# Turns in two sequence mixers: transposes in place of products with the identity

## The chip, the cores and the metric

The kernel runs on one core of one Trainium2 chip. The metric is the device time of one execution in microseconds. The kernel before took 2492.74 us (median of 3 runs, 2491.64 to 2497.43).

## What is computed

Two transformer blocks, one behind the other, on 256 tokens of width 2048, all in float32. The first block's middle part is a pair of recurrent mixers; the second block's is an attention with a forget gate. Only the first block's mixers matter here:

```python
def first_block(x, ...):
    h = rms_norm(x, attn_norm_w[l])
    proj = h @ w_cat                                   # 2048 -> 6448
    y_a, v_first = rwkv7_mixer(p_rwkv, ...)            # 16 heads of 64
    y_b = gdn_mixer(p_gdn, ...)                        # 8 value heads of 128, 4 key heads
    y = jnp.concatenate([y_a, y_b], axis=-1)
    x = x + y @ w_out[l]
    h = rms_norm(x, ffn_norm_w[l])
    x = x + (silu(h @ ffn_w_gate[l]) * (h @ ffn_w_up[l])) @ ffn_w_down[l]
```

The first mixer keeps for each head a 64 x 64 state that every token updates:

```python
def step(S, inp):                                      # rwkv7_recurrence
    Sa = einsum('bhvk,bhk->bhv', S, a_t)
    S = S * w_t + Sa[..., None] * b_t + v_t[..., None] * k_t
    return S, einsum('bhvk,bhk->bhv', S, r_t)
```

The second is the gated delta rule in chunks of 64 tokens: `v_new = u - w @ S`, `o = q_g @ S + A_qk @ v_new`, `S = S * exp(g_last) + k_g.T @ v_new`, where `u` and `w` solve a unit lower triangular system `L + I` of 64 x 64. The kernel computes both mixers in chunks of 64 tokens, with products and an inverse of such a triangular matrix in place of the token by token scan.

## The kernel before

Activations lie channel by channel on the 128 partitions, with the 256 tokens along the free axis. The large products (`unit`, L1921; its three products are L1952 to L1954) stream all weights once from memory through a ring of 4 slots; each weight is split by ScalarE (L606) and VectorE (L1076) in a high and a low part, and three products make one. Their phases are: input projection (to about 305 us), mixers (305 to 545 us), output projection, FFN, then the second block. Each engine runs its own program in written order; semaphores join them.

Inside the mixers the weight slots are used as work space and TensorE runs many small products. Two heads of 64 channels share a tile of 128 partitions: `halves_of` (L2092) holds the slices 0 to 63 and 64 to 127, and most small products are issued as a pair, one for each half. `C` is 64, `P` 128, `T` 256, `PAIRS` 8 (pairs of heads of the first mixer), `NCH` 4 (chunks), `G_QK` 4 (key heads of the second).

The chunk algorithm needs many 64-token blocks turned (channels to tokens or back). A turn is a product with the identity matrix `ident`: the block is the stationary operand, `ident` the moving one, and the result lands in PSUM. The turns, in the order in which TensorE comes to them:

- the fills: `chunk_tokens` (L2094, product at L2097) turns values, b and k of a chunk, 12 calls of 8 pairs; `chunk_turn` (L2109, product at L2113) turns the start of the inverse, 4 calls of 8 pairs. The list `FILLS` mixes these calls with `chunk_scores` (L2106, a real product) over the 8 PSUM banks, each fill waiting for the bank's eviction eight fills earlier;
- five levels of the first inverse (L2144, L2152, L2156), no turns;
- the first mixer's scan over 4 chunks (L2194 to L2243), into which `value_tokens` (L2172) is woven in chunks 1 and 2: 4 pairs a call, each pair reading all 128 partitions and writing one half;
- the turn of `GT` at L2249 (16 pairs), then five levels of the second inverse (L2259, L2275, L2279), with `key_tokens` (L2165) in four of them and `value_tokens` in two, 4 pairs a call;
- `turned_heads` (L2289), the first mixer's output back to channels, 4 calls of 8 pairs: two ahead of the second mixer's scan, two in its first step;
- `turned_values` (L2312), the second mixer's output back, 4 calls of 4 full 128 x 128 blocks, in steps 2 and 3 of that scan and behind it.

ACT evicts most turns (L820, L824, L841, L864, L888); each call signals once, on its last instruction. Elsewhere in the kernel (x at the start L2012, small vectors L2007 and L2026, the attention L2414 and L2422, the end L2459) blocks are turned by `nc.tensor.transpose`, which takes the same operands.

Of the kernel before, what the change touches and what calls it, by code (L numbers as in the profile page):

```python
# [24 lines left out]
P = 128  # L25
T = 256
# [3 lines left out]
C = 64  # L30
# [13 lines left out]
INV_BANKS, SIDE_BANKS = (7, 1, 5, 0), (2, 6, 4, 3)  # L44
STATE_BANKS, O_BANKS, TURN_BANKS, Y_BANKS = (1, 5), (7, 4), (6, 3), (2, 6, 3, 2)
# [40 lines left out]
def build(nc, io, out):  # L86
    with ExitStack() as ctx:
# [39 lines left out]
        ident = at("ident", [P, P], o); o += 512  # L127
# [52 lines left out]
        YT = at("YT", [P, NCH, PAIRS, C], a3 + 16384)  # L180
# [14 lines left out]
        TT = at("TT", [P, SLOTS, C], w0)  # L195
# [20 lines left out]
        QC, KC, VC = QKVC[:, 0:4, :], QKVC[:, 4:8, :], QKVC[:, 8:16, :]  # L216
# [11 lines left out]
        GT = at("GT", [P, NCH, 2, G_QK, C], w0)  # L228
# [10 lines left out]
        OT = at("OT", [P, NCH, G_QK, P], a3 + 8192)  # L239
# [37 lines left out]
        ps = [ctx.enter_context(nc.psum_tensor(f"ps{i}", [P, 512], F32)) for i in range(8)]  # L277
# [1637 lines left out]
        def _(pe):  # L1915
            mm = nc.tensor.matmul
# [86 lines left out]
            for n in range(NT):  # L2003
# [5 lines left out]
                for q in range(4):  # L2009
                    for i in range(4):  # L2010
                        f = 4 * q + i
                        ins = nc.tensor.transpose(ps[4 * n + q][:, i * P:(i + 1) * P], XIN[:, n, f * P:(f + 1) * P],  # L2012
                                                  ident[:])
                    ins.then_inc(S("x_turned"), 1)

            for j in range(4):
                if j == 3:
                    pe.wait_ge(S("vecs_landed"), counts["vecs_landed"])
                    for i, pack in list(enumerate(PACKS))[1:]:
                        r = sum(n for _, n in pack)  # L2020
                        b = 3 + (i - 1) % 5
# [15 lines left out]
            for name, r, b0 in (("w_lora", slice(0, 64), 0), ("a_lora", slice(64, 128), 4)):  # L2037
                for t in range(PAIRS):
                    pe.wait_ge(bank_freed, N_OUT - 8 + b0 + t // 2 + 1 + FREE_BANKS)
                    ins = mm(ps[b0 + t // 2][:, (t % 2) * T:(t % 2 + 1) * T], WA_UP[r, t * P:(t + 1) * P],  # L2040
                             PR[r, T_WA, PAD:TP], start=True, stop=True)
# [27 lines left out]
            for t in range(PAIRS):  # L2069
                o_ = ps[4 + t // 2][:, (t % 2) * T:(t % 2 + 1) * T]  # L2070
                mm(o_, G_UP[:, 0, t * P:(t + 1) * P], PR[:, T_G0, PAD:TP], start=True, stop=False)
                ins = mm(o_, G_UP[:, 1, t * P:(t + 1) * P], PR[:, T_G1, PAD:TP], start=False, stop=True)
# [5 lines left out]
            for c in range(NCH):  # L2078
                for e, rr in enumerate((slice(0, C), slice(C, P))):
                    ins = mm(ps[0][rr, 16 * c:16 * c + 16], ROWS[:, c * C:(c + 1) * C], picks[:, e, :, 0, :],  # L2080
                             start=True, stop=True)
# [9 lines left out]

            halves_of = (slice(0, C), slice(C, P))  # L2092

            def chunk_tokens(dst, src, c):  # L2094
                for t in range(PAIRS):
                    for rr in halves_of:
                        ins = mm(dst[rr, t * C:(t + 1) * C], src[rr, t, c * C:(c + 1) * C], ident[rr, rr],  # L2097
                                 start=True, stop=True)
                ins.then_inc(S("tok_turned"), 1)

            def chunk_scores(dst, src, q):
# [7 lines left out]
            def chunk_turn(dst, c):  # L2109
                got("tt_started")  # L2110
                for t in range(PAIRS):
                    for rr in halves_of:
                        ins = mm(dst[rr, t * C:(t + 1) * C], TT[rr, 8 * c + t, :], ident[rr, rr], start=True, stop=True)  # L2113
                ins.then_inc(S("tm_turned"), 1)

            k_hat, v_in = (PR[:, t:t + PAIRS, PAD:TP] for t in (T_K, T_V))
# [2 lines left out]
            for fill, kind in enumerate(FILLS):  # L2119
# [4 lines left out]
                dst, i = ps[fill % 8], place[kind]  # L2124
# [12 lines left out]
            for lev in range(1, 6):  # L2137
                for b in range(NCH):
# [3 lines left out]
                    for t in range(PAIRS):  # L2142
                        for rr in halves_of:
                            ins = mm(ps[2 * b][rr, t * C:(t + 1) * C], LO[rr, 8 * b + t, :], TM[rr, 8 * b + t, :],  # L2144
                                     start=True, stop=True)
                    ins.then_inc(S("inv_p"), 1)
                for b in range(NCH):
                    got("inv_pm")
                    if lev < 5:
                        for t in range(PAIRS):  # L2150
                            for rr in halves_of:
                                mm(ps[2 * b][rr, t * C:(t + 1) * C], TT[rr, 8 * b + t, :], PM[rr, 8 * b + t, :],  # L2152
                                   start=True, stop=True)
                    for t in range(PAIRS):
                        for rr in halves_of:
                            ins = mm(ps[2 * b + 1][rr, t * C:(t + 1) * C], PM[rr, 8 * b + t, :], TT[rr, 8 * b + t, :],  # L2156
                                     start=True, stop=True)
# [4 lines left out]
            def key_tokens(c, b):  # L2162
                for a in range(G_QK):
                    for rr in halves_of:
                        ins = mm(ps[b][rr, a * P:(a + 1) * P], KC[:, a, c * C:(c + 1) * C], ident[:],  # L2165
                                 start=True, stop=True)
                ins.then_inc(S("tok_turned"), 1)

            def value_tokens(c, b):
                for a in range(G_QK):  # L2170
                    for e, rr in enumerate(halves_of):
                        ins = mm(ps[b][rr, a * P:(a + 1) * P], VC[:, 2 * a + e, c * C:(c + 1) * C], ident[:],  # L2172
                                 start=True, stop=True)
                ins.then_inc(S("tok_turned"), 1)

            def gram(c):
# [6 lines left out]
            for c in range(NCH):  # L2183
                cc = slice(c * C, c * C + C)
                s0 = ST[:, c % 2]
                for hb in range(2):
                    if c:
                        got("s_out")
                    for i in range(4):
                        t = 4 * hb + i  # L2190
# [4 lines left out]
                        for rr in halves_of:  # L2195
                            ins = mm(o_[rr], LKR[rr, 8 * c + t, 0, :], VTOK[rr, 8 * c + t, :], start=c == 0, stop=True)
# [11 lines left out]
                for hb in range(2):  # L2208
# [3 lines left out]
                    for i in range(4):  # L2212
                        t = 4 * hb + i
                        for rr in halves_of:
                            ins = mm(ps[2 + 4 * hb][rr, i * C:(i + 1) * C], TT[rr, 8 * c + t, :], R1[rr, t, :],
                                     start=True, stop=True)
                    ins.then_inc(S("u_summed"), 1)
                for hb in range(2):
# [3 lines left out]
                    for i in range(4):  # L2222
                        t = 4 * hb + i
# [3 lines left out]
                        for rr in halves_of:  # L2227
                            ins = mm(o_[rr], BTOK[rr, 8 * c + t, :], UU[rr, t, :], start=False, stop=True)
# [6 lines left out]
                for t in range(PAIRS):  # L2235
# [6 lines left out]
                    for rr in halves_of:  # L2242
                        ins = mm(o_[rr], LBR[rr, 8 * c + t, 1, :], UU[rr, t, :], start=False, stop=True)  # L2243
                ins.then_inc(S("y_summed"), 1)
            for c in range(NCH):
                got("gtt_start")
                for a in range(G_QK):
                    for rr in halves_of:
                        ins = mm(ps[INV_BANKS[c]][rr, a * C:(a + 1) * C], GT[rr, c, 1, a, :], ident[rr, rr],  # L2249
                                 start=True, stop=True)  # L2250
                ins.then_inc(S("tm_turned"), 1)

            for lev in range(1, 6):
                for c in range(NCH):
                    got("inv_off")
                    got("inv_added" if lev > 1 else "tm_made")
                    for a in range(G_QK):
                        for rr in halves_of:
                            ins = mm(ps[INV_BANKS[c]][rr, a * C:(a + 1) * C], gLO[rr, c, a, :], GT[rr, c, 0, a, :],  # L2259
                                     start=True, stop=True)  # L2260
# [8 lines left out]
                for c in range(NCH):  # L2269
                    got("inv_pm")  # L2270
                    b = INV_BANKS[c]
                    if lev < 5:
                        for a in range(G_QK):
                            for rr in halves_of:
                                mm(ps[b][rr, a * C:(a + 1) * C], GT[rr, c, 1, a, :], gPM[rr, c, a, :],  # L2275
                                   start=True, stop=True)
                    for a in range(G_QK):
                        for rr in halves_of:
                            ins = mm(ps[b][rr, T + a * C:T + (a + 1) * C], gPM[rr, c, a, :], GT[rr, c, 1, a, :],  # L2279
                                     start=True, stop=True)  # L2280
# [4 lines left out]
            def turned_heads(e):  # L2285
                for t in (2 * e, 2 * e + 1):
                    for k in range(NCH):
                        for rr in halves_of:
                            ins = mm(ps[Y_BANKS[e]][rr, (t % 2) * T + k * C:(t % 2) * T + (k + 1) * C],  # L2289
                                     YT[rr, k, t, :], ident[rr, rr], start=True, stop=True)  # L2290
                ins.then_inc(S("y_turned"), 1)
            for c in range(NCH):
                got("inv_added")
                for a in range(G_QK):
                    for rr in halves_of:
                        ins = mm(ps[INV_BANKS[c]][rr, a * P:(a + 1) * P], GT[rr, c, 1, a, :], VB[rr, c, a, :],
                                 start=True, stop=True)
# [11 lines left out]
            def turned_values(c):  # L2309
                got("o_out")  # L2310
                for a in range(G_QK):
                    ins = mm(ps[TURN_BANKS[c % 2]][:, a * P:(a + 1) * P], OT[:, c, a, :], ident[:], start=True, stop=True)  # L2312
                ins.then_inc(S("o_turned"), 1)

            def state_sums(c, vn):
# [29 lines left out]
            for c in range(1, NCH):  # L2345
                vn = VN[:, c % 2, :, :]
                got("gs_out", 2)
                for a in range(G_QK):
                    for e, rr in enumerate(halves_of):
                        ins = mm(ps[0][rr, a * P:(a + 1) * P], WT[:, c, e, a, :], gS[c % 2][:, 4 * e + a, :],  # L2350
                                 start=True, stop=True)
# [126 lines left out]
```

## Time and profile before

| | |
|---|---|
| median of 3 runs | 2492.74 us (2491.64 to 2497.43) |
| the profiled execution | 2492.21 us, of which the span of the profile 2490.4 us |
| TensorE busy (MATMUL) | 2436.8 us, 98% of the span, 24650 records |
| VectorE, ScalarE, GpSimd busy | 59%, 45%, 5% |
| mean granted TensorE clock | 0.995 of full |
| memory traffic | 431.72 MB, 173 GB/s |

Times are those of one profiled execution, in us unless marked ns. PE is TensorE's MATMUL, PEld its weight load, DVE VectorE, ACT ScalarE, POOL GpSimd. A FP32 product shows as two MATMUL records, each with a load of its own. "64*128 64x64" is the form of a record: 64 rows and 128 columns of the array hold the stationary operand, and a moving operand of 64 partitions x 64 elements goes through. Ends of MATMULs are modelled and overlap the next one's start, so rates are read from starts: in a row of the timeline, "start us, us" is the first start and the time to the last end. PEclk 1.00 is 2.4 GHz.

### The profile page before, as it was taken

Reading aid. Unit: us, or ns where it says so; the run is one execution under the profiler, and the core shown is the slowest. Engines: PE = TensorE matmul, PEld = TensorE weight load, DVE = VectorE, ACT = ScalarE, POOL = GpSimd, SP = SyncE. Lnnn points to the kernel's source line nnn. Section 1 sums busy time; section 2 is a strip of 40 time slices with the busy share of each in tenths; the row PEclk is TensorE's granted clock in tenths of the full one; section 3 lists DMA queues with packets and bytes.
Section 4 is the critical chain, followed back from the end, with each engine's and each line's share of the span. In section 5 each row is a group of like instructions: output and inputs, shape, how many; then the busy total and the mean of one; then the engine's idle time right before and its main releaser. Section 6 shows DMA issues by size and latency. Waiting matters only on the chain.

```text
span 2490.4 us, 57362 instructions
## 1 busy us (share of the span) xinstructions
PE 2436.8 (98%) x24650; PEld 2409.6 (97%) x24650; DVE 1477.9 (59%) x1683; ACT 1122.8 (45%) x1061; POOL 114.4 (5%) x93
## 2 busy tenths in 40 slices
PE   8999979989999999999999999999999999999999
PEld 8999968989999999999999999989999999999998
DVE  5557598664654545554445567675576666765444
ACT  4333524444544444443344544363555555544332
POOL 3000050000200000000020100000200000000000
PEclk9999989999999999999999999999999999999999
DMA  7555300126555655556665565626565565656664
GB/s 233 186 188 199 119 2 4 37 86 186 194 195 188 198 186 194 193 189 196 189 197 192 186 237 202 218 78 197 187 196 192 189 198 186 196 191 190 198 188 150
DMA packets 171387, 431.72 MB, mean 173 GB/s; under 512 B 17614, under 2 KB 23387, under 8 KB 170107
## 3 DMA queue, kind: packets, MB, share of 16 engines
q1 hardware_dynamic: 170027, 422.30, 52.3%
q10 hardware_dynamic: 1232, 7.52, 0.8%
q8 instruction: 104, 1.70, 0.3%
q14 instruction: 24, 0.20, 0.0%
HBM read 427.59 MB, written 2.17 MB: 173 GB/s over the span
## 4 chain that ended last, share of the span: by engine, by line
PE 92%; DVE 6%; ACT 1%; POOL 1%; issue 0%; DMA 0%; DVEq 0%; SPq 0%; ACTq 0%; POOLq 0%
PE ps L1952 29%; PE ps L1953 29%; PE ps L1954 29%; PE ps L2106 1%; POOL SQ L528 1%; DVE TM L1351 0%; DVE LO L1355 0%; DVE TT L1352 0%; DVE CV L1385 0%; ACT HIW L606 0%; DVE LOW L1076 0%; DVE GT L1367 0%; PE ps L2144 0%; DVE TMP L1298 0%; PE ps L2050 0%
## 5 line engine op out<-in xcount | busy, mean ns | idle before, releaser
L1076 DVE TENSOR_TENSOR LOW<-RAW,HIW 128x2048 fp32r<-128x2048 f32 (+1 forms) x397 | 912.8, 2299 | 916.4 <-ACT HIW L606 916.3
L1952 PE MATMUL ps<-H_ROWS,HIW 128*128 128x256 f32 x4928 | 1369.1, 278 | 6.3 <-DVE LOW L1076 3.6
L1953 PE MATMUL ps<-H_ROWS,HIW 128*128 128x256 f32 x4928 | 1368.0, 278 | 0.0
L1954 PE MATMUL ps<-H_ROWS,LOW 128*128 128x256 f32 x4928 | 1367.1, 277 | 0.0
L606 ACT ACTIVATE HIW<-RAW 128x2048 fp32r<-128x2048 f32 (+1 forms) x397 | 760.9, 1917 | 1182.7 <-PE ps L1954 1178.2
L1952 PEld LDWEIGHTS ps<-H_ROWS,HIW 128*128 128x128 f32 x4928 | 927.9, 188 | 7.6 <-DVE LOW L1076 4.0
L1954 PEld LDWEIGHTS ps<-H_ROWS,LOW 128*128 128x128 f32 x4928 | 929.2, 189 | 0.0
L1953 PEld LDWEIGHTS ps<-H_ROWS,HIW 128*128 128x128 f32 x4928 | 927.5, 188 | 0.1
L1952 PE MATMUL ps<-HID,HIW 128*128 (+1 forms) x1408 | 389.3, 276 | 0.0
L1953 PE MATMUL ps<-HID,HIW 128*128 (+1 forms) x1408 | 389.2, 276 | 0.0
L1954 PE MATMUL ps<-HID,LOW 128*128 (+1 forms) x1408 | 389.1, 276 | 0.0
L1952 PEld LDWEIGHTS ps<-HID,HIW 128*128 128x128 f32 x1408 | 264.4, 188 | 0.2 <-issue 0.2
L1954 PEld LDWEIGHTS ps<-HID,LOW 128*128 128x128 f32 x1408 | 264.4, 188 | 0.0
L1953 PEld LDWEIGHTS ps<-HID,HIW 128*128 128x128 f32 x1408 | 264.4, 188 | 0.0
L528 POOL TENSOR_TENSOR NSQ<-NSQ 128x1024 f32<-128x1024 f32 (+2 forms) x12 | 26.2, 2187 | 502.9 <-ACT NSQ L634 502.3
L1896 DVE SCALAR_TENSOR_TENSOR YV<-UC,vec,YV 128x256 f32<-128x256 f32 x88 | 42.5, 483 | 0.0
L1896 DVE SCALAR_TENSOR_TENSOR YG<-UC,vec,YG 128x256 f32<-128x256 f32 x88 | 42.5, 483 | 0.0
L528 POOL TENSOR_TENSOR SQA<-SQA 128x1024 f32<-128x1024 f32 (+1 forms) x4 | 9.8, 2460 | 603.7 <-ACT SQA L640 603.6
L1120 DVE TENSOR_TENSOR UC<-ps,rstd 128x256 f32<-128x256 f32 x88 | 30.1, 418 | 0.0
L648 ACT ACTIVATE H_ROWS<-X,vec 128x256 fp32r<-128x256 f32 x64 | 27.0, 494 | 0.0
L1115 DVE SCALAR_TENSOR_TENSOR H_ROWS<-X,vec,H_ROWS 128x256 fp32r<-128x256 f32 x64 | 26.8, 479 | 0.0
L1045 ACT ACTIVATE YV<-UC,vec 128x256 f32<-128x256 f32 x44 | 25.9, 588 | 0.0
(365 smaller groups left out, 1507.0 us busy)
## 6 DMA issues: line engine op xcount, KB each, us to landing
RAW<-in_ffn_w_up SPq DMA_DIRECT2D x264, 512.0 KB, 4.5
RAW<-in_ffn_w_down SPq DMA_DIRECT2D x176, 512.0 KB, 4.8
RAW<-in_fox_w_in SPq DMA_DIRECT2D x98, 512.0 KB, 4.6
RAW<-in_w_in SPq DMA_DIRECT2D x96, 512.0 KB, 4.2
RAW<-in_ffn_w_gate SPq DMA_DIRECT2D x88, 512.0 KB, 3.8
RAW<-in_w_out SPq DMA_DIRECT2D x32, 512.0 KB, 5.0
RAW<-in_fox_w_out SPq DMA_DIRECT2D x32, 512.0 KB, 4.7
INV<-rows_out ACTq DMA_DIRECT2D x4, 1024.0 KB, 7.2
```

The costliest lines, as they stand in the source:

```text
L528: tick(nc.gpsimd.tensor_tensor(sq[:, 0:n, :], sq[:, 0:n, :], sq[:, n:2 * n, :], ALU.add), "pool_step")
L606: A(HIW[:, u_const % 2, 0:n], RAW[:, u_const % 4, 0:n], ACT.Copy).then_inc(hi_made, 1)
L648: A(H(0, f, f + 1)[:, 0, :], X[:, f, :], ACT.Copy, scale=vec[:, c + f:c + f + 1]).then_inc(S("h_hi"), 1)
L1045: ins = A(conv_out(i), UC[:, i, 0:T], ACT.Identity, scale=conv_tap(g, 0, i), bias=vec[:, bass.ds(g * 4 + (cb + (i % 2) * FT + i // 2), 1)])
L1076: V.tensor_tensor(LOW[:, u_const % 4, 0:n], RAW[:, u_const % 4, 0:n], HIW[:, u_const % 2, 0:n].bitcast(F32), ALU.subtract).then_inc(lo_mad ...
L1115: V.scalar_tensor_tensor(H(1, f, f + 1)[:, 0, :], X[:, f, :], vec[:, c + f:c + f + 1], H(0, f, f + 1)[:, 0, :].bitcast(F32), ALU.mult, ALU ...
L1120: return V.tensor_tensor(dst, ps[f][:, 0:T], rstd[:], ALU.mult)
L1896: ins = V.scalar_tensor_tensor(conv_out(i), UC[:, i, j - 1:j - 1 + T], conv_tap(g, j - 1, i), conv_out(i), ALU.mult, ALU.add)
L1952: mm(o_, hi_w, h_hi, start=start, stop=False)
L1953: mm(o_, hi_w, h_lo, start=False, stop=False)
L1954: i = mm(o_, lo_w, h_hi, start=False, stop=stop)
L2106: ins = mm(dst[rr, i * P:(i + 1) * P], src[rr, t, cc], AR[rr, t, :, cc], start=True, stop=True)
```

## The change

Every turn of the mixers' main part whose result starts at partition 0 becomes `nc.tensor.transpose`; its partner, which lands on partitions 64 to 127, stays a product. The second mixer's turned values, which are full blocks, all become transposes. Nothing else is moved; the operands, the order, the waits and the signals stay. (`picks`, `spread_inverse` and the real products are untouched.)

```diff
+            def turned(dst, src, rr, unit_matrix):
+
+                if rr.start == 0:
+                    return nc.tensor.transpose(dst[rr], src, unit_matrix)
+                return mm(dst[rr], src, unit_matrix, start=True, stop=True)
+
             def chunk_tokens(dst, src, c):
                 for t in range(PAIRS):
                     for rr in halves_of:
-                        ins = mm(dst[rr, t * C:(t + 1) * C], src[rr, t, c * C:(c + 1) * C], ident[rr, rr],
-                                 start=True, stop=True)
+                        ins = turned(dst[:, t * C:(t + 1) * C], src[rr, t, c * C:(c + 1) * C], rr, ident[rr, rr])
                 ins.then_inc(S("tok_turned"), 1)
...
-                        ins = mm(dst[rr, t * C:(t + 1) * C], TT[rr, 8 * c + t, :], ident[rr, rr], start=True, stop=True)
+                        ins = turned(dst[:, t * C:(t + 1) * C], TT[rr, 8 * c + t, :], rr, ident[rr, rr])
...
-                        ins = mm(ps[b][rr, a * P:(a + 1) * P], KC[:, a, c * C:(c + 1) * C], ident[:],
-                                 start=True, stop=True)
+                        ins = turned(ps[b][:, a * P:(a + 1) * P], KC[:, a, c * C:(c + 1) * C], rr, ident[:])
...
-                        ins = mm(ps[b][rr, a * P:(a + 1) * P], VC[:, 2 * a + e, c * C:(c + 1) * C], ident[:],
-                                 start=True, stop=True)
+                        ins = turned(ps[b][:, a * P:(a + 1) * P], VC[:, 2 * a + e, c * C:(c + 1) * C], rr, ident[:])
...
-                        ins = mm(ps[INV_BANKS[c]][rr, a * C:(a + 1) * C], GT[rr, c, 1, a, :], ident[rr, rr],
-                                 start=True, stop=True)
+                        ins = turned(ps[INV_BANKS[c]][:, a * C:(a + 1) * C], GT[rr, c, 1, a, :], rr, ident[rr, rr])
...
-                            ins = mm(ps[Y_BANKS[e]][rr, (t % 2) * T + k * C:(t % 2) * T + (k + 1) * C],
-                                     YT[rr, k, t, :], ident[rr, rr], start=True, stop=True)
+                            ins = turned(ps[Y_BANKS[e]][:, (t % 2) * T + k * C:(t % 2) * T + (k + 1) * C],
+                                         YT[rr, k, t, :], rr, ident[rr, rr])
...
             def turned_values(c):
                 got("o_out")
                 for a in range(G_QK):
-                    ins = mm(ps[TURN_BANKS[c % 2]][:, a * P:(a + 1) * P], OT[:, c, a, :], ident[:], start=True, stop=True)
+                    ins = nc.tensor.transpose(ps[TURN_BANKS[c % 2]][:, a * P:(a + 1) * P], OT[:, c, a, :], ident[:])
                 ins.then_inc(S("o_turned"), 1)
```

## Rows read from the trace of the kernel before

**Rows 1.** The page, part 1: busy time and share of the span.

```profile
PE 2436.8 (98%) x24650; PEld 2409.6 (97%) x24650; DVE 1477.9 (59%) x1683; ACT 1122.8 (45%) x1061; POOL 114.4 (5%) x93
```

**Rows 2.** The page, part 4: the chain that ended last, by engine.

```profile
PE 92%; DVE 6%; ACT 1%; POOL 1%; issue 0%; DMA 0%; DVEq 0%; SPq 0%; ACTq 0%; POOLq 0%
```

**Rows 3.** That chain in order of time, 335 to 565 us: start us, us, what.

```profile
360.13 1.15 PE ps L2097 x32
...
367.58 3.75 PE ps L2113 x128
...
443.43 1.02 PE ps L2172 x16
...
472.43 1.87 PE ps L2249 x64
...
476.17 1.02 PE ps L2165 x16
...
484.49 0.87 PE ps L2172 x16
...
518.19 2.01 PE ps L2289 x64
...
521.22 2.01 PE ps L2289 x64
```

**Rows 4.** TensorE's waits, 339 to 372 us: total us, times, longest.

```profile
PE ps L2097 <- DVE LKR L1441: 0.6, 1, 0.6
```

**Rows 5.** Single lines of TensorE: min/median/max ns, first and last start, forms.

```profile
L2097 PE MATMUL ps<-ident,PR x256: 215/218/268, 348.4 to 366.5; 64*64 64x64 f32 x128
...
L2289 PE MATMUL ps<-ident,YT x128: 217/219/268, 518.1 to 523.0; 64*64 64x64 f32 x128
...
L2165 PE MATMUL ps<-ident,PR x64: 272/273/323, 476.1 to 500.4; 128*64 128x128 f32 x64
```

**Rows 6.** The same for the full-width turn L2312 and for two transposes.

```profile
L2312 PE MATMUL ps<-ident,OT x32: 274/275/377, 527.6 to 544.1; 128*128 128x128 f32 x32
...
L2422 PE MATMUL ps<-ident,SC x48: 272/273/329, 1640.1 to 1669.5; 128*128 128x128 f32 x48
...
L2026 PE MATMUL ps<-ident,VPACK x7: 223/272/297, 29.2 to 30.4; 88*128 88x88 f32 x4, 67*128 67x67 f32 x1, 83*128 83x83 f32 x1, 64*128 64x64 f32 x1
```

**Rows 7.** Timeline of TensorE: start us, us to the last end, instructions.

```profile
483.40 1.09 PE L2165 MATMUL ps<-ident,PR 128*64 128x128 f32 x16
484.32 1.04 PE L2172 MATMUL ps<-ident,PR 128*64 128x128 f32 x16
485.30 0.68 PE L2275 MATMUL ps<-gPM,GT 64*64 64x64 f32 x16
...
515.16 1.09 PE L2331 MATMUL ps<-U,AL 64*64 64x128 f32 x16
516.18 2.00 PE L2304 MATMUL ps<-GT,KBE 64*128 64x64 f32 x32
518.12 2.08 PE L2289 MATMUL ps<-ident,YT 64*64 64x64 f32 x64
```

**Rows 8.** The same timeline at the end of the mixers; in brackets the idle time before.

```profile
539.19 1.16 PE L2312 MATMUL ps<-ident,OT 128*128 128x128 f32 x8 [0.33 <-ACT OT L888]
543.23 1.16 PE L2312 MATMUL ps<-ident,OT 128*128 128x128 f32 x8 [2.88 <-ACT OT L888]
```

**Rows 9.** Three stretches: length, busy by engine, PEclk, DMA share, GB/s.

```profile
348.30:372.00 23.70, 22.41 (x646) 22.13 (x642) 21.25 (x36) 10.28 (x17) 12.07 (x9) 1.00 0.02 4
541.50:544.90 3.40, 1.16 (x8) 0.97 (x8) 1.95 (x6) 3.07 (x10) 0.00 (x0) 1.00 0.00 0
544.90:551.70 6.80, 6.02 (x28) 6.03 (x29) 3.97 (x6) 1.90 (x3) 0.00 (x0) 0.50 0.00 0
```

**Rows 10.** Timeline of TensorE at the start: 16 transposes twice.

```profile
6.26 3.27 PE L2012 MATMUL ps<-ident,XIN 128*128 128x128 f32 x16 [6.26 <-DMA XIN<-in_x]
...
9.62 1.97 PE L2012 MATMUL ps<-ident,XIN 128*128 128x128 f32 x16
```

## The prediction

> **What bounds the kernel now.** I read the page's busy shares first, then the chain of work that ended last, then that chain in order of time through the two mixers of the first block (335 to 545 us), and only then single lines. TensorE is busy for 98% of the span [rows 1] and carries 92% of the chain [rows 2]; nearly all of that is the large products, which the change does not touch. What it touches lies in the mixers. There the reader should see in the chain that the turns are on it almost everywhere: the fills (L2097, L2113), the value and key turns (L2172, L2165), the turn of GT (L2249) and both pairs of head turns (L2289) [rows 3]. In the fills, 339 to 372 us, TensorE stood idle only once behind its first start, 0.6 us on a DVE mask product [rows 4]. So a nanosecond more or less on a turn is a nanosecond of the kernel, and the price of one turn decides.
>
> **How a pair of turns runs today.** A turn comes as a pair: the half on partitions 0 to 63 and the half on 64 to 127. Each product is two MATMUL records (16 products of a call give 32 records), and its form is 64*64: 64 rows, 64 columns of the array [rows 5]. One 128-wide record of L2312 follows the next after (1.16 - 0.28 - 0.10) / 7 = 0.11 us (1.16 us for 8 records, less the tail of the last, 0.275, and what the first is longer than the median, 0.377 - 0.275 [rows 6, 8]), so a 64-wide one should take 0.055. But L2113 runs 128 records in 3.75 us, 0.029 each [rows 3]: the two halves, in opposite corners of the array, run at the same time. A narrow pair costs 4 x 0.029 = 0.117 us, set equally by either half. A wide pair (L2165, L2172: form 128*64, 128 moving columns) costs 0.217: 0.87 us for the four of a call [rows 3].
>
> **What the change does to a pair.** The lower half becomes one transpose, the upper stays a product. Counts: 8 pairs in each of 12 token fills and 4 TT turns (128 pairs), 16 in GT, 32 in the heads: 176 narrow. The wide ones are 4 pairs in 8 calls: 32. Each loses one MATMUL and one weight load of four.
>
> First, the length of a transpose. Sixteen transposes at the start take 1.97 us [rows 10]: less the last one's tail (0.273) and the first one's extra (0.055) that is 0.11 us each, against 0.22 for a product of that size in two records. It saves half. (The Trainium skill, "TensorE: Matmul & The Clock Gate", section Terms, calls transpose mode four times faster for FP32; the rows disagree, showing a factor of two. By the page a narrow transpose would take 0.027 instead of 0.055, and the sum below would be 6.5 us less.)
>
> But halving one half alone wins nothing even in the best case: the upper half still needs its two records of 0.055, and they set the pace of a pair that runs side by side. The lower bound of a pair is thus about 0.11, as now.
>
> Second, and this decides: can it still run side by side? No row shows a transpose that uses fewer than 128 columns of the array. The forms are 128*128, 88*128, 83*128, 67*128, and even the one with 64 rows and a 64x64 moving matrix is 64*128 [rows 6]; all of them had 128 stationary columns, so this is a hint and no proof. The helper's own condition is the second hint: it transposes only where the output starts at partition 0. An operation that could live in a 64*64 corner could live in either; one that takes the full width can only start at the left edge. I take the new instruction as 64*128 (128*128 in the wide turns), so it alternates with products of form 64*64 (128*64). (The Trainium skill, "TensorEngine Tiling (Array Packing)", Restrictions, says the same: column tiling disables transpose mode for FP32 input. No row here can confirm it.)
>
> Third, what alternating between forms costs. The timeline of TensorE has such changes, now only between calls. L2172 starts at 484.32 and L2275, another form, at 485.30: 0.98 us for four pairs that cost 0.87, where nothing is waited for, so about 0.10 for leaving the form. L2165 before it, which changes the form on entry and not at its end, takes 0.92: 0.05 for the first load that nothing hides [rows 7]. The medians agree: the first record after a change is 0.05 longer (268 against 218, 323 against 272 [rows 5]). The pair of forms that matters here is there too: L2331 (64*64) gives way to L2304 (64*128) after 1.02 us for four pairs of 0.217, again 0.15 over [rows 7]. So a change costs 0.15 in all: 0.10 to empty the array and 0.05 for the load. (The same page of the Trainium skill, Key Properties, says that changing the tiling mode drains TensorE; the trace agrees, and has the price that the page lacks.) Before a transpose the bare load is cheaper: 128 columns are 0.055 longer (329 against 273) where a product's are 0.10 (377 against 275) [rows 6]; for 64 columns I take 0.027.
>
> A narrow pair afterwards, start to start: transpose 0.027 load + 0.055 + 0.10 to empty = 0.182; first product record 0.05 + 0.055 = 0.105; second 0.055 + 0.10 = 0.155. Sum 0.44 against 0.117: **+0.325 us**. A wide pair, with 0.11 in place of 0.055: 0.237 + 0.16 + 0.21 = 0.607; a call of four 2.43 against 1.02 [rows 3], **+1.40 us**.
>
> **The sum.**
> - Fills (L2097, L2113): 128 x 0.325 = 41.6, less the 0.6 us of idle time that swallows the start of it [rows 4]: +41.0. The ACT and DVE evictions behind each fill keep their length and have more time.
> - Turn of GT: 16 x 0.325 = +5.2. On the chain as a whole [rows 3].
> - Key and value turns: 8 x 1.40 = +11.2. L2172 at 443 and 452 us lies in a stretch where TensorE has no gap; in the levels of the inverse TensorE goes from these calls straight on to L2275 without waiting, so it was the later one and the delay passes on.
> - Head turns: 32 x 0.325 = 10.4, less the 0.15 by which each of the two stretches' entries is a change of form already: +10.1.
> - Second mixer's turned values: 16 products of 0.22 become transposes of 0.11, -0.44 us of TensorE in each of four calls, -1.8 in all. These are full width, with no alternation. But L2312 is nowhere on the chain; before two of the calls TensorE has stood idle for ACT, 2.88 us before the last [rows 8]. I price it at 0. If all were exposed it would be 1.8.
>
> No wait is added, the signal of each call stays on its last instruction, and no DMA or queue moves. Sum: 41.0 + 5.2 + 11.2 + 10.1 = **+67.5 us**. On the profiled execution (2492.2 us, of which 2490.4 span) that is 2559.7; the median of the runs is 0.5 above it, so **2560 us**.
>
> Bounds of the pair, the one unknown price: from below 0.055 x 3 = 0.165 (in turn, but without emptying the array): 176 x 0.048 + 32 x 0.11 = +12 us in all; if a transpose loads as slowly as a full product (0.10) the pair is 0.51 and the sum 13 us more. Nearest are the L2331 to L2304 rows, which have the very two forms.
>
> **Rivals.**
> 1. *The clock falls in the turns.* The granted clock was 1.00 from 348 to 372 us with TensorE nearly gapless; it was 0.50, the 1.2 GHz level, in 544.9 to 551.7, right behind a stretch with 2.2 us idle out of 3.4 [rows 9]. The new stretches have no gap so long, but the array streams in only 3 x 0.055 of each 0.44 us and stands empty otherwise; no row shows such a pattern. The stretches are 176 x 0.44 + 32 x 0.61 = 97 us long, so at the half clock throughout they would cost up to 97 more; half of that gives 2608, all of it 2657. (The Trainium skill, "TensorE: Matmul & The Clock Gate", Part 4, says that transposes do not bring the full clock at all. The trace disagrees: 16 transposes alone in 3.27 us, then the same number in 1.97 [rows 10].) Chance 20%.
> 2. *In turn, but no emptying.* For: the changes of form in the rows are all between different calls. Against: four of them cost the same. 2493 + 12 = 2505. Chance 6%.
> 3. *Side by side after all*, the other side. If the chip runs the transpose in a 64*64 corner, the upper product hides it; decided by whether the record's form has 64 columns. Then the pair is 0.11 as now and only turned values differ: 2491 to 2493. Chance 8%.
> 4. *The turn gets cheaper by the instructions it loses*, 3 of 4: 176 x 0.029 + 32 x 0.054 + 1.8 = 8.6 less, 2484. (The Trainium skill, "Perfetto Trace Analysis", section Transposes, advises a transpose for any logical transposition, as it skips the arithmetic.) Against: both halves would have to share one resource, which 0.029 per record denies. Chance 3%.
>
> **How the numbers follow.** The forecast holds 63%, with a range of its own of 2538 to 2575. The whole range, 2530 to 2630, takes in the lower seven tenths of rival 1 and leaves out rivals 2 to 4. What a measurement can tell from no change is 0.3%, 7.5 us: faster by more 3%, within it 8%, slower by more 89%.
>
> **What would show it.** Right: a form of 64*128 (128*128) at the transposes; MATMUL records of a token fill in a row T, product, product, with starts about 0.18, 0.105 and 0.155 apart; a fill of L2097's kind taking 3.5 us for 0.93; the first block's large products behind the mixers starting some 67 us later and all behind it unchanged. Wrong: forms of 64*64 and fills of 0.93 us (rival 3); 1.3 us (rival 2); PEclk under 1 between 340 and 600 us in more slices than before (rival 1). A gain where L2312 runs would say that I misread the tail.

## The result and the profile after

The changed kernel takes 2598.73 us (median of 4 runs, 2593.35 to 2603.38) against 2492.19 for the kernel before beside it: 1.041 times as long, 95% interval 1.0387 to 1.0433, or +106.5 us where +67.5 was forecast. The profiled execution took 2593.35 us, its span is 2591.6.

The page answers [rows 1] with the first of these lines and [rows 2] with the last; between them is the granted clock in 40 slices, in which the kernel before has one digit under 9, an 8, and this one a 7, a 5 and an 8:

```profile
PE 2539.6 (98%) x24426; PEld 2463.4 (95%) x24426; DVE 1478.2 (57%) x1683; ACT 1123.6 (43%) x1061; POOL 114.4 (4%) x93
...
PEclk9999975998999999999999999999999999999999
...
PE 93%; DVE 5%; ACT 1%; POOL 1%; issue 0%; DMA 0%; DVEq 0%; SPq 0%; ACTq 0%; POOLq 0%
```

TensorE has 224 records fewer and 103 us more of busy time. The changed lines now are L2097 (the transpose) and L2098 (its partner). Where the time went, the same seven stages show: fills, first inverse, first scan (with two wide calls and the turn of GT), second inverse (six wide calls), heads and second scan, then everything up to the attention, and the rest. Columns: stretch, length, TensorE busy (records), PEclk, DMA share, GB/s. The kernel before:

```profile
339.40:372.20 32.80, 31.31 (x769) 0.94 0.01 3
372.20:435.20 63.00, 57.44 (x1808) 1.00 0.02 4
435.20:474.10 38.90, 35.48 (x1057) 1.00 0.10 34
474.10:508.70 34.60, 33.24 (x1002) 1.00 0.08 31
508.70:545.70 37.00, 29.63 (x503) 0.99 0.32 115
545.70:1635.80 1090.10, 1089.89 (x9526) 1.00 0.60 195
1635.80:2484.90 849.10, 844.40 (x7380) 1.00 0.56 180
```

The changed kernel:

```profile
338.60:439.40 100.80, 99.90 (x640) 0.57 0.00 1
439.40:504.50 65.10, 59.52 (x1810) 0.97 0.02 4
504.50:553.60 49.10, 45.68 (x1031) 0.93 0.12 46
553.60:598.00 44.40, 43.04 (x971) 0.97 0.01 3
598.00:651.30 53.30, 45.13 (x456) 0.78 0.22 80
651.30:1737.40 1086.10, 1085.89 (x9527) 1.00 0.59 196
1737.40:2586.40 849.00, 844.30 (x7379) 1.00 0.53 180
```

The fills lengthened by 68.0 us, the first inverse, which the change does not touch, by 2.1 (some of it at the half clock), the first scan and the second inverse by 10.2 and 9.8, the heads' stage by 16.3. The stages behind gave 4.1 back and the start 0.8; why was not looked into. That makes up the 101 us between the two profiled executions. Where the stages behind the fills grew by more than their pairs, part of them ran at the half clock as well: their mean clock is 0.97, 0.93, 0.97 and 0.78, against 0.99 or more before.

A pair of turns reads in the timeline of TensorE as T (one record) and its partner (two). First at the full clock, then, in the same fills, at the half:

```profile
348.01 0.24 PE L2097 MATMUL ps<-ident,PR 64*64 64x64 f32 x1
348.18 0.33 PE L2098 MATMUL ps<-ident,PR 64*64 64x64 f32 x2
348.44 0.24 PE L2097 MATMUL ps<-ident,PR 64*64 64x64 f32 x1
...
358.21 0.47 PE L2098 MATMUL ps<-ident,PR 64*64 64x64 f32 x2
358.61 0.31 PE L2097 MATMUL ps<-ident,PR 64*64 64x64 f32 x1
358.85 0.47 PE L2098 MATMUL ps<-ident,PR 64*64 64x64 f32 x2
```

Start to start that is 0.43 us a pair (0.17 to the partner, 0.26 for it), against the forecast's 0.44; at the half clock 0.64 (0.24 and 0.40). Most of the fills ran at the half clock:

```profile
341.00:355.10 14.10, 14.10 (x176) 0.98 0.01 2
355.10:443.80 88.70, 87.82 (x530) 0.50 0.00 1
```

### The profile page after: what moved, and what is told of

Its sections match the earlier page's. It is cut to its first block, busy times and chain, and to the rows that moved or that the text cites. A ratio compares the mean times of both kernels' runs of the same rounds, so it can differ in the third digit from the quotient of the medians.

```text
span 2591.6 us, 56914 instructions
## 1 busy us (share of the span) xinstructions
PE 2539.6 (98%) x24426; PEld 2463.4 (95%) x24426; DVE 1478.2 (57%) x1683; ACT 1123.6 (43%) x1061; POOL 114.4 (4%) x93
## 4 chain that ended last, share of the span: by engine, by line
PE 93%; DVE 5%; ACT 1%; POOL 1%; issue 0%; DMA 0%; DVEq 0%; SPq 0%; ACTq 0%; POOLq 0%
PE ps L1952 27%; PE ps L1953 27%; PE ps L1954 27%; PE ps L2098 3%; PE ps L2097 2%; PE ps L2111 1%; POOL SQ L528 1%; DVE TM L1351 0%; DVE LO L1355 0%; DVE TT L1352 0%; DVE CV L1385 0%; PE ps L2149 0%; ACT HIW L606 0%; DVE LOW L1076 0%; DVE GT L1367 0%
## 5 line engine op out<-in xcount | busy, mean ns | idle before, releaser
L2098 PE MATMUL ps<-ident,PR 64*64 64x64 f32 (+1 forms) x192 | 41.5, 308 | 0.0
L1441 DVE TENSOR_TENSOR LKR<-ps,upper_c 128x512 f32<-128x512 f32 x8 | 5.5, 692 | 51.8 <-PE ps L2111 51.8
L2098 PEld LDWEIGHTS ps<-ident,PR 64*64 64x64 f32 (+1 forms) x192 | 22.6, 166 | 10.4
```

Source lines behind the costliest of these rows:

```text
L1441: V.tensor_tensor(dst, src, many(upper2_c[:].rearrange("p a t -> p (a t)"), 4), ALU.mult)\
L2098: return mm(dst[rr], src, unit_matrix, start=True, stop=True)
```

## Which part costs what

Four kernels, each with a part of the change, the rest left as products.

**Turned values alone** (`e1_values_only`): the kernel before with this line.

```diff
-ins = mm(ps[TURN_BANKS[c % 2]][:, a * P:(a + 1) * P], OT[:, c, a, :], ident[:], start=True, stop=True)
+ins = nc.tensor.transpose(ps[TURN_BANKS[c % 2]][:, a * P:(a + 1) * P], OT[:, c, a, :], ident[:])
```

> The kernel before with only the turned values of the second mixer as transposes (16 instructions of the whole array, in four calls); everything else is as before. Theory of the changed array form: no change of form is added, since the neighbours of these calls are the same as before, so the time stays within 1.8 us of the kernel before (0 to 1.8 us faster). Rival, that the transposing mode in itself costs an emptying of the array at its start and its end: 8 emptyings of 0.1 us, all of them on the chain, 1 us slower. With so small a price for either, the rows of the four calls decide: 8 records 0.11 apart before, 4 records 0.11 apart after.

Measured: 2490.89 us (12 runs) against 2492.87; ratio 0.9988, interval 0.9976 to 1.0. The four calls in its timeline, in brackets the idle time before, answer [rows 8]:

```profile
532.08 0.66 PE L2312 MATMUL ps<-ident,OT 128*128 128x128 f32 x4 [0.23 <-DVE GATE L1530]
538.70 0.66 PE L2312 MATMUL ps<-ident,OT 128*128 128x128 f32 x4
543.65 0.66 PE L2312 MATMUL ps<-ident,OT 128*128 128x128 f32 x4 [0.34 <-ACT OT L888]
547.69 1.12 PE L2312 MATMUL ps<-ident,OT 128*128 128x128 f32 x4 [3.38 <-ACT OT L888]
```

The products that follow the first two calls, in this kernel:

```profile
534.53 1.16 PE L2318 MATMUL ps<-VN,KG 64*128 64x128 f32 x16 [1.80 <-DVE VN L1561]
...
541.20 1.09 PE L2327 MATMUL ps<-gS,QG 128*64 128x128 f32 x16 [1.85 <-DVE VN L1561]
```

In the kernel before, the first call (of the four, [rows 8] shows the last two) and the same products:

```profile
527.62 1.16 PE L2312 MATMUL ps<-ident,OT 128*128 128x128 f32 x8 [0.23 <-DVE GATE L1530]
530.08 1.16 PE L2318 MATMUL ps<-VN,KG 64*128 64x128 f32 x16 [1.30 <-DVE VN L1561]
...
536.74 1.09 PE L2327 MATMUL ps<-gS,QG 128*64 128x128 f32 x16 [1.35 <-DVE VN L1561]
```

The first three calls each shrank from 1.16 to 0.66 us, yet the first and the fourth start 15.61 us apart in both kernels (532.08 and 547.69; 527.62 and 543.23). What TensorE saved went into its next wait: behind the first two calls the wait for VectorE's `VN` grew by 0.50 us each (1.30 to 1.80, 1.35 to 1.85), behind the third the wait for ScalarE's `OT` (2.88 to 3.38). The fourth call took 1.12 us for 1.16, as its stretch (547.6 to 549.0 us) has a granted clock of 0.50, where the same call of the kernel before (543.2 to 544.5) has 1.00. It isn't on the chain at either length: `OG` (L1586), the VectorE operation that takes its result, starts when VectorE is done with `H_ROWS` (L1593, L1595), at 549.04 us here and 544.58 before, 0.23 and 0.19 us behind the turns' end. So the price of 0 in the sum stands.

**Fills, late narrow pairs, wide pairs alone.** Each passes the other calls to the old product:

```diff
+as_product = lambda dst, src, rr, unit_matrix: mm(dst[rr], src, unit_matrix, start=True, stop=True)
+turned_fill = transposed    # or as_product
+turned_wide = as_product    # or transposed
+turned_late = as_product    # or transposed
```

> Of the change only the fills of the first mixer (128 pairs: 96 of tokens and 32 of the inverse's start); all other turns and the turned values stay products. Theory: these pairs carry their cost alone and the clock falls inside them, not because of what the rest of the change does. Then the stretch of the fills is again 101 us for 33, most of it at the half clock, and the kernel takes 2492 + 68 = 2560 us. Rival, that the clock fell as an outcome of the whole change: the fills stay at the full clock, 33 + 41 = 74 us, and the kernel takes 2533 us.

Measured: 2567.32 us, ratio 1.029 (1.0264 to 1.0317). Its fills have the length and the clock of the whole change's, 101.1 us at a PEclk of 0.57 (100.8 at 0.57).

> Of the change only the narrow pairs after the fills: 16 of the second mixer's inverse and 32 of the heads. Theory, by the pair's price of 0.32 us at the full clock (0.44 less 0.117) and the stages of the changed kernel: the inverse's pairs +5, the heads' stage +16 (of which 22 us at the half clock), 2492 + 21 = 2513 us. Rival, that the half clock in the heads' stage was carried over from what the wide turns had done ahead of it: the stage gains 10 us only and the kernel takes 2507.

Measured: 2517.87 us, ratio 1.0097 (1.0073 to 1.0121). The heads' stage gains 17 us (54.4 for 37.0) and has a mean clock of 0.77 (0.78 in the whole change), with no wide turn changed in the kernel: the fall was not carried over from them.

> Of the change only the 32 wide pairs, in 8 calls. Theory: a call takes 2.43 us for 1.02 at the full clock, all of it on the chain, 8 x 1.4 = 11 us: 2503 us; where the half clock comes with it, up to 2508. Rival, that the calls lie in the shadow of the side work of the inverse's levels: 2493 to 2497.

Measured: 2503.93 us (10 runs), ratio 1.0039 (1.0024 to 1.0053). Its timeline has wide pairs 0.59 us apart (forecast 0.607), and the scan and inverse that hold the 8 calls grew by 2.7 and 8.3 us, at the full clock:

```profile
434.20:475.80 41.60, 38.18 (x1051) 1.00 0.10 32
475.80:518.70 42.90, 41.54 (x974) 1.00 0.07 24
...
478.34 0.30 PE L2097 MATMUL ps<-ident,PR 128*64 128x128 f32 x1
478.57 0.43 PE L2098 MATMUL ps<-ident,PR 128*64 128x128 f32 x2
478.93 0.30 PE L2097 MATMUL ps<-ident,PR 128*64 128x128 f32 x1
```

The parts add up: about 74 + 25 + 11 = 110 us for 106.5 of the whole. The wide pairs alone cost what the forecast gave them (11.2). What it missed lies in the narrow ones, which ran largely at the half clock.

## What makes a pair three times as long: the width or the mode?

The twin kernels have the same 100 narrow pairs of the fills changed, and nothing else. In one the lower half is a transpose; in the other it is `wide_product`, an ordinary product (`mm`) whose stationary operand is two neighbouring blocks, 128 columns. From the first twin to the second, in `chunk_tokens` (`chunk_turn` likewise):

```diff
 if rr.start == 0 and c < NCH - 1:
-    nc.tensor.transpose(o_[rr], src[rr, t, c * C:(c + 1) * C], ident[rr, rr])
+    wide_product(o_, src[rr, t, c * C:(c + 2) * C], ident[rr, rr])
```

> The kernel before with transposes as the lower half of exactly the 100 pairs in which its twin has products of full width. Theory: 100/128 of what the fills alone cost (they cost 74 us), 58 us slower than before, 2550; from the pair's price at the full clock alone, 32 us slower, 2525. It is the measure for the twin: equal times speak for the width, a twin that is much faster for the transposing mode.

Measured: 2545.8 us, ratio 1.0207 (1.017 to 1.0245).

> The kernel before, no transposes added. In 100 of the 128 pairs of the first mixer's fills (token turns of the first three chunks of each kind, and seven of eight pairs of each of the inverse's four calls) the lower half is an ordinary product with the identity whose weights are 64 rows by 128 columns, two neighbouring blocks; the second block lands on the upper partitions, where the upper half's own product then writes over it. So the lower record takes the whole width of the array, as the transpose seems to, but in the ordinary mode. Theory of the changed form (width makes the two halves exclude each other and empties the array between them): a pair costs about what a transposed pair costs, 0.43 us at the full clock and 0.64 at the half, so the kernel is 32 to 52 us slower than before and equals its twin with transposes in the same 100 places. Rival, that the transposing mode makes the emptying and the width only excludes: four records of 0.053 in a row, 0.21 us a pair, 9 us slower than before.

Measured: 2590.47 us, ratio 1.0393 (1.0354 to 1.0433): no transpose in the mixers, and 45 us more than with transposes in the same places; equal times, as expected, they are not. The timeline at the full clock:

```profile
349.08 0.43 PE L2099 MATMUL ps<-ident,PR 64*128 64x64 f32 x2
349.44 0.33 PE L2108 MATMUL ps<-ident,PR 64*64 64x64 f32 x2
349.69 0.43 PE L2099 MATMUL ps<-ident,PR 64*128 64x64 f32 x2
350.06 0.32 PE L2108 MATMUL ps<-ident,PR 64*64 64x64 f32 x2
350.31 0.43 PE L2099 MATMUL ps<-ident,PR 64*128 64x64 f32 x2
```

From the partner's first record to the next wide product it is 0.25 us, as behind a transpose (0.26); from the wide product to its partner 0.36 to 0.37, 0.19 more than from a transpose (0.17), as it has a second record and a dearer load. That, 100 times and largely at the half clock, is why this twin is the slower one (fills of 121.0 us for 83.2). Record and load account for some 0.13 of the 0.19 (0.055, and 0.10 for 0.027 in the prediction's terms); the wide product also writes its second block where the partner writes next, and whether the rest comes from that no run separates. The way back, 0.25 us, has no such overlap. So the rival, four records in a row at 0.21 us, falls: the emptying comes with the width. That the mode brings none of its own, rows of full-width work show, where transposes (L2416, L2424) stand next to products of the same width (L2435, changed kernel): 0.43 us for 4, 0.33 for 3, 0.11 each, with nothing between.

```profile
1745.16 0.60 PE L2416 MATMUL ps<-ident,QKV 128*128 128x128 f32 x4
1745.59 0.49 PE L2424 MATMUL ps<-ident,SC 128*128 128x128 f32 x3
1745.92 0.39 PE L2435 MATMUL ps<-PT,VT 128*128 128x128 f32 x2
```

A transpose whose record reads 64*64 behaves beside a 64*64 product like an operation of the whole width. That it occupies the whole width is the reading that fits all of these rows; it is inferred, since the record itself names only the columns that hold data, and no run has the transposing mode change between operations of half the width alone.

## Is it each transpose, or each change?

The changed kernel in another order: in each call first g lower halves, then their g partners.

```diff
+def in_groups(n):                                  # g = 2, 4 or 8
+    return [(x, rr) for x0 in range(0, n, g) for rr in halves_of for x in range(x0, min(n, x0 + g))]
...
-for t in range(PAIRS):
-    for rr in halves_of:
-        ins = turned(...)
+for t, rr in in_groups(PAIRS):
+    ins = turned(...)
```

> The changed kernel with the same instructions in another order: in each call first all lower halves (transposes), then all upper halves (products), 8 pairs to a group (4 in the wide calls). Theory, that the price sits in the changes of form: a group of g narrow pairs costs 2 emptyings and their first loads once, about 0.28 + 0.165 g us, so 0.20 us a pair for g = 8 where alternation costs 0.43; with 0.117 before, the narrow pairs cost 176 x 0.083 = 15 us and the wide ones 2 to 5, and the array is dense enough to keep the full clock: 2508 to 2515 us. Rival, that a transpose is slow in itself: 0.18 + 0.155 = 0.34 us a pair whatever the order, 2492 + 176 x 0.22 + 11 = 2542 us or more.

> The same in groups of 4. Theory of the changes of form: 0.28 + 0.165 x 4 = 0.94 us, 0.234 a pair, 176 x 0.117 = 21 us and 3 to 5 for the wide pairs, 2517 us with the full clock, 2540 with the half one. Together with the groups of 1, 2 and 8 it shows at which length the half clock appears.

> The changed kernel, lower halves (transposes) and upper halves (products) in groups of 2. Theory of the changes of form: a group costs 0.28 + 0.165 x 2 = 0.61 us, 0.30 a pair, so 176 x 0.19 = 33 us over before with the full clock and 5 for the wide pairs, 2530 us; if the clock still falls as it does for single pairs, the emptyings take no longer but the records do, 0.47 a pair, 2560 us. Rival of the slow transpose: 0.34 a pair or more whatever the group.

| pairs in a group | a pair at the full clock (0.20 to 0.30 worked out) | fills of the profiled execution | PEclk in them | median, us | ratio (interval) |
|---|---|---|---|---|---|
| before, side by side | 0.117 | 32.8 | 0.94 | 2492 | 1 |
| 8 | 0.20 | 43.3 | 0.95 | 2512.18 | 1.008 (1.0057 to 1.0103) |
| 4 | 0.234 | 48.2 | 0.92 | 2540.93 | 1.0191 (1.0163 to 1.0218) |
| 2 | 0.30 | 79.5 | 0.59 | 2562.56 | 1.0287 (1.0254 to 1.032) |
| 1, the change | 0.43 | 100.8 | 0.57 | 2598.73 | 1.041 (1.0387 to 1.0433) |

```profile
351.71 0.63 PE L2100 MATMUL ps<-ident,PR 64*64 64x64 f32 x8
352.27 1.14 PE L2101 MATMUL ps<-ident,PR 64*64 64x64 f32 x16
353.35 0.64 PE L2100 MATMUL ps<-ident,PR 64*64 64x64 f32 x8
```

In the groups of 8 (rows above) eight pairs take 353.35 - 351.71 = 1.64 us, 0.205 each; the fills grew by 10.5 us for the 10.6 of the formula. The rival of a transpose that is slow in itself, 2542 us whatever the order, falls. Even the best order loses: a transpose and its partner one after the other need 0.165 us without any change of form, more than the 0.117 of two products side by side. In groups of 4 the kernel has two times: 2529.91 us in the profiled execution, and 2540.5 to 2541.4 in the three others, with a mean clock of 0.982 for 0.991. By these means that is an estimated 46 us more at the half clock for 11 us more of time, of the same program. The profiled one kept the full clock through most of its fills (1.00 from 345 to 384 us) and then fell too, to 0.50 up to 394 us; with other short falls behind that is, by the mean clocks (0.991 for 0.995), an estimated 20 us more at the half clock than in the kernel before, and some 10 of the 13 us by which it lies above the 2517 expected. (The 0.94 of the kernel before is a stretch at 0.50 that ends at 343.7 us, ahead of the first turn; the other kernels of the table have one there as well.)

## What brings the half clock?

**More transposes between two changes.**

```diff
 if rr.start == 0:
+    for _ in range(2):
+        nc.tensor.transpose(dst[rr], src, unit_matrix)
     return nc.tensor.transpose(dst[rr], src, unit_matrix)
```

> The changed kernel with each transposed lower half issued three times in a row (the same values to the same place), 416 more transposes. Theory, that the clock falls because the array idles between changes of form: the repeats fill the array without new changes, the half clock in the fills shrinks from 87 us to little, and a pair takes 0.43 + 2 x 0.055 = 0.54 us, less than the 0.64 it takes now at the half clock: the fills take about 33 + 128 x 0.42 = 87 us for 101, and the kernel is 5 to 20 us faster than the changed one although it does more. Rival, that alternation of forms itself brings the half clock, or that transposes do not count as work for it: the half clock stays, a pair takes about 0.64 + 0.22 = 0.86 us, the fills 130 us, the kernel 2640 us.

Measured: 2638.74 us, ratio 1.058 (1.0541 to 1.0619), the fills 127.7 us at PEclk 0.55. A pair took 0.54 us before the clock fell and 0.86 afterwards. The rival's numbers, 0.86, 130 and 2640, fit all three: repeated transposes do not keep the clock up.

**More products between two changes**: the same with the partner, three and seven times.

```diff
+for _ in range(2):                                 # 6 in the kernel with seven
+    mm(dst[rr], src, unit_matrix, start=True, stop=True)
 return mm(dst[rr], src, unit_matrix, start=True, stop=True)
```

> The changed kernel with each upper half (a product) issued three times in a row, the same values to the same place, and the transposes once. The twin with repeated transposes kept the half clock. Theory, that ordinary products hold the clock up and transposes or the waits between forms don't: the full clock comes back, a narrow pair takes 0.43 + 4 x 0.053 = 0.64 us (as much as it takes now at the half clock with 4 records fewer), the fills 100 us, the kernel 2590 to 2605 us. Rival, that the alternation itself brings the half clock whatever stands between: 0.64 + 4 x 0.107 = 1.07 us a pair, the fills 155 us, the kernel 2660 to 2680 us.

> The changed kernel with each upper half (a product) issued seven times in a row, the transposes once. As many changes of form as in the changed kernel, but more products between two of them than in the kernel with three. Rival that has held so far, that the alternation itself brings the half clock whatever stands between: a narrow pair takes (0.43 + 12 x 0.053) = 1.07 us at the full clock and about 0.64 + 12 x 0.107 = 1.92 us at the half, so the fills 33 + 128 x 1.8 = 263 us and the kernel some 2820 us. Theory, that it is the array's standing still at the changes, as a part of all time, that brings it: with enough products between them the full clock comes back although the changes are as many: the fills take 33 + 128 x 0.95 = 155 us, as in the kernel with three, and the kernel about 2690 us.

Measured: 2686.92 us with three (ratio 1.077, 1.074 to 1.08), 2868.37 with seven (1.1513, 1.1477 to 1.1549). Both went to the half clock and stayed there to the end of the fills. The fills have the lengths that the rival gave (155 and 263 us). The kernels are slower than it said, by 7 us with three products and 48 with seven; with seven, the wide pairs account for most of that: they take 1.90 us each in its timeline (681.03 to 688.64 for four), an estimated 53 us over before for all 32, where they cost 11 in the changed kernel. The fills of the two, and a pair of the second at either clock:

```profile
341.80:498.80 157.00, 156.16 (x1152) 0.53 0.00 1
```

```profile
339.50:605.70 266.20, 265.31 (x2178) 0.52 0.00 1
350.59 0.24 PE L2097 MATMUL ps<-ident,PR 64*64 64x64 f32 x1
350.76 0.91 PE L2099 MATMUL ps<-ident,PR 64*64 64x64 f32 x12
351.51 0.28 PE L2100 MATMUL ps<-ident,PR 64*64 64x64 f32 x2
351.72 0.24 PE L2097 MATMUL ps<-ident,PR 64*64 64x64 f32 x1
...
369.95 0.31 PE L2097 MATMUL ps<-ident,PR 64*64 64x64 f32 x1
370.19 1.54 PE L2099 MATMUL ps<-ident,PR 64*64 64x64 f32 x12
371.52 0.42 PE L2100 MATMUL ps<-ident,PR 64*64 64x64 f32 x2
371.87 0.31 PE L2097 MATMUL ps<-ident,PR 64*64 64x64 f32 x1
```

My theory for both, that products fill the array and bring the full clock back, was wrong twice. Nor does the number of changes in a time explain it: the kernel with seven has two changes in 1.13 us (350.59 to 351.72) and lost the clock; the one in groups of 4 has two in 0.94 and kept it for most of its fills in one execution. What differs besides is how little of the long fills is left to calls whose products run in both corners at once: `chunk_scores`, and in the twin kernels the token calls of the fourth chunk, whose eight pairs stayed products. The traces lean towards these. Each twin came back to the full clock for some 3 us three times within its fills (at 363.6, 384.1 and 404.5 us with transposes, at 374.6, 402.0 and 432.4 without), each time within 3.3 us of the start of such a token call, while the changed kernel, which has none, never came back in its fills. And the groups of 4 lost the clock at 384.2 us, 5.5 us into the four calls of `chunk_turn` (378.72 to 388.5), the only ones with no `chunk_scores` between them. But no run varied this alone, and the cause of the fall **stays open**.

Shown is that it comes with these turns, in the fills and in the heads' stage each by itself; that it takes no transposes, as the twin with products of full width has a PEclk of 0.58 in 121.0 us of fills; that neither repeated transposes nor repeated products prevent it; and that with groups of 8 the fills and the head turns keep the full clock.

## Why the prediction was right, and where it was short

- **In short.** The sum's 2560 us with its own range of 2538 to 2575 missed: 2599. The whole range of 2530 to 2630 held, by rival 1. The mechanism of the pair was right; the term at fault is the clock.
- **What bounds it: right.** Each turn of the mixers was on the chain, and the stages grew by what their pairs grew. The wide pairs, deepest in other work, cost 11.0 us for 11.2.
- **The pair: right, 0.43 for 0.44 narrow, 0.59 for 0.607 wide.** Term by term: transpose to partner 0.17 (0.182), the rest 0.26 (0.26). The reason, width and not mode, held in the twin kernels; the 0.10 us of emptying from L2172 to L2275 and L2331 to L2304 [rows 7] was the right row to go by. Rivals 2, 3 and 4 fell with it.
- **The sign I gave for it: wrong.** I expected records of form 64*128 (128*128), and said that 64*64 would mean rival 3. They read 64*64 and 128*64, and the two halves still did not overlap. The form tells the columns that hold data; the starts were the criterion, 0.17 and 0.26 us.
- **The turned values: right** at 0; three calls' savings went into waits for VectorE and ScalarE, and the last call lies in the shadow of VectorE's own work.
- **The clock: the term that was missing.** The sum took the full clock; rival 1 had 20%. It came true in the fills (PEclk 0.57) and the heads' stage (0.78), and less in the turn of GT, whose last pairs ran at 0.50 (549.8 us on). Fills 68.0 for 41.0: 27 us. Heads' stage 16.3 for 10.1: 6. Scan and second inverse 20.0 for 16.4, the first inverse 2.1 for 0. Together 39, less the 4.9 given back elsewhere, 34 us above the forecast in the profiled execution (101.1 for 67.5); the medians lie 39 above.
- **Rival 1's size: too large.** It doubled a pair at the half clock, 0.88 us. Measured is 0.64: of the steps, 0.17 became 0.24 and 0.26 became 0.40, so part of the time between forms does not follow the clock. "Half of that, 2608" would be by these numbers 2560 + (176 x 0.21 + some) / 2, about 2580, and the whole some 2600. The kernel landed at 2599 with nearly all of the fills and much of the heads at the half clock: inside the range, for the right reason at the wrong price, and with a chance that was too small. That it landed well inside is partly luck: at the price stated, 0.44 us more a pair, fills and heads alone (160 pairs) would give 2560 + 70 = 2630, the very edge. The prediction named the warning itself, a pattern that no row showed.
- **[Rows 10], read against this rival.** The two stretches of transposes do differ in pace, 0.21 and 0.11 us each, but the granted clock reads 1.00 in both (6.2 to 8.8 and 9.6 to 11.4 us). That the clock rose in them is inferred from the pace; the record of the clock doesn't show it.

## What to carry to other kernels

Two small products in opposite corners of the array cost the time of one (0.117 us a pair here); before replacing one of them by a cheaper instruction, ask whether the new one still fits beside the other, and price the two changes of form that it brings if not (0.12 and 0.15 us here: 0.17 and 0.26 less records of 0.055 and 0.107). Read whether two operations overlap from the starts of their records, not from their form. If operations of two forms must be mixed, put all of one form ahead of all of the other (0.205 us a pair for 0.43), and watch the granted clock of the stretch: here it added 34 us to a direct loss of 67 in the profiled execution.

## What was not expected of the hardware

- Stretches of alternating forms, without idle time to speak of, fell from the full clock to the 1.2 GHz level some 8 us after the first pair (347.1 to 355.1) and stayed there for 88.7 us; with seven products in each pair, for 256 us. With products alone, one of full width in each pair, it fell too.
- At that level a pair took 1.49 times as long (0.64 for 0.43), the large share of products in the kernel with seven 1.70 times (1.92 for 1.13).
- One program can keep the clock longer or lose it sooner from run to run: 2529.91 us at a mean of 0.991 or 2541 at 0.982 in groups of 4.
